# A one-input copy for GpSimd's first weight pass, and the residual stream renewed by VectorE alone

## The reference

```python
# layer 0: Mamba-2 SSD mixer, then an MLP
z, xbc, dt = split(rmsnorm(h, g_pre) @ w_in)        # 2048 | 3072 | 32 columns
xbc = silu(causal_conv4(xbc))                       # depthwise, 4 taps
y, state = ssd(xbc, dt)                             # chunked for the prompt, one step per sample
g = group_rmsnorm((y + x * d) * silu(z)) * gate
h = h + rmsnorm(g @ w_out, g_post)
h = h + rmsnorm(relu(rmsnorm(h, g_pre) @ w_up) ** 2 @ w_down, g_post)
# shared keys and values, once
k, v = split(rmsnorm(h, g_kv) @ w_kv); k = rope(k)
# layer 1: differential attention with its own queries, then an MLP of the same form
h = h + rmsnorm(subln(attn(q, k, v)) @ w_o, g_post)
h = h + rmsnorm(relu(rmsnorm(h, g_pre) @ w_up) ** 2 @ w_down, g_post)
```

## Time and profile before

| | |
|---|---|
| median of 3 runs | 1827.74 us (1825.21 to 1828.12) |
| profiled execution | 1827.72 us |
| its span, first to last instruction | 1825.9 us |
| mean granted clock of TensorE, share of full | 0.923 |
| busy: PE, DVE, ACT, POOL | 1577.9, 1266.2, 469.1, 1332.7 us |
| HBM read, written | 142.07 MB, 16.16 MB |

### The profile page before, as it was taken

One profiled execution on the slowest core, in us unless ns is written; L12 is line 12 of the kernel. 1 busy time (PEld: TensorE's weight loads), 2 busy tenths in 40 slices (PEclk: granted clock), 3 DMA queues, 4 the chain that ended last, 5 costly groups with the idle time before them and its releaser, 6 DMA issues.

```text
span 1825.9 us, 29727 instructions
## 1 busy us (share of the span) xinstructions
PE 1577.9 (86%) x11978; PEld 1479.8 (81%) x11978; DVE 1266.2 (69%) x1075; ACT 469.1 (26%) x1158; POOL 1332.7 (73%) x586
## 2 busy tenths in 40 slices
PE   5999888876499699999997699976769799999995
PEld 5999656876489699999997599953349799999995
DVE  6899888799941698018845936998862996038645
ACT  3433322555621321002100311125542321002100
POOL 5878588556568789888887766644418788888885
PEclk8999999988699799999999799978879799999997
DMA  4222000244423133333333123442212133323321
GB/s 146 75 83 85 18 6 12 105 173 150 150 58 92 47 91 86 92 89 92 92 93 104 45 60 116 135 179 93 70 47 81 47 92 91 92 87 91 92 90 47
DMA packets 44151, 159.40 MB, mean 87 GB/s; under 512 B 5026, under 2 KB 5410, under 8 KB 43810
## 3 DMA queue, kind: packets, MB, share of 16 engines
q1 hardware_dynamic: 44066, 158.25, 27.4%
HBM read 142.07 MB, written 16.16 MB: 87 GB/s over the span
## 4 chain that ended last, share of the span: by engine, by line
PE 55%; DVE 32%; issue 6%; ACT 3%; POOL 2%; DMA 1%; SPq 0%; DVEq 0%; POOLq 0%; ACTq 0%
PE GP L495 17%; PE GP L497 17%; PE GP L496 17%; DVE cacc L1274 4%; DVE hT L1376 2%; DVE acc L1396 2%; DVE hc L1336 2%; DVE hs L1333 2%; DVE kq L1473 1%; DVE aL L1371 1%; DVE hs L1330 1%; DVE decay L1293 1%; DVE misc L1517 1%; DVE hst L1305 1%; DVE yss L1337 1%
## 5 line engine op out<-in xcount | busy, mean ns | idle before, releaser
L405 POOL TENSOR_TENSOR wH<-wraw,cst 128x1024 fp32r<-128x1024 f32 x216 | 532.7, 2466 | 325.6 <-PE GP L497 315.4
L495 PE MATMUL GP<-aH,wH 128*128 128x260 f32 x1920 | 559.9, 292 | 89.4 <-DVE aL L1371 35.2
L409 POOL TENSOR_TENSOR wL<-wraw,wH 128x1024 fp32r<-128x1024 f32 x216 | 576.4, 2668 | 17.0
L497 PE MATMUL GP<-aH,wL 128*128 128x260 f32 x1920 | 553.5, 288 | 0.0
L496 PE MATMUL GP<-aL,wH 128*128 128x260 f32 x1920 | 552.8, 288 | 0.0
L495 PEld LDWEIGHTS GP<-aH,wH 128*128 128x128 f32 x1920 | 373.3, 194 | 98.3 <-issue 49.6
L495 PE MATMUL GP<-hidH,wH 128*128 128x260 f32 x1536 | 440.8, 287 | 8.0 <-DVE hidL L1347 7.3
L497 PE MATMUL GP<-hidH,wL 128*128 128x260 f32 x1536 | 435.9, 284 | 0.0
L496 PE MATMUL GP<-hidL,wH 128*128 128x260 f32 x1536 | 434.9, 283 | 0.0
L496 PEld LDWEIGHTS GP<-aL,wH 128*128 128x128 f32 x1920 | 373.8, 195 | 0.1
L497 PEld LDWEIGHTS GP<-aH,wL 128*128 128x128 f32 x1920 | 373.4, 194 | 0.0
(11 more groups left out here) (255 smaller groups left out, 2041.9 us busy)
## 6 DMA issues: line engine op xcount, KB each, us to landing
wraw<-wblk SPq DMA_DIRECT2D x216, 512.0 KB, 3.6
hs<-ssm_in SPq DMA_DIRECT2D x16, 512.0 KB, 3.7
sssm<-hs SPq DMA_DIRECT2D x16, 512.0 KB, 2.8
ktile<-kcache SPq DMA_DIRECT2D x16, 512.0 KB, 3.6
vtile<-vcache SPq DMA_DIRECT2D x16, 512.0 KB, 4.5
hT<-x_t SPq DMA_DIRECT2D x4, 520.0 KB, 5.1
kt_out<-kT SPq DMA_DIRECT2D x1, 2080.0 KB, 6.6
vt_out<-vT SPq DMA_DIRECT2D x1, 2080.0 KB, 10.6
```

The source lines that it names most:

```text
L405: pool.tensor_tensor(wH[:, d, :].rearrange("p (k n) -> p k n", k=8), raw[:, s, :].rearrange("p (k n) -> p k n", k=8), cst[:, C_ONE:C_ONE + ...
L409: pool.tensor_tensor(wL[:, d, :], raw[:, s, :], wH[:, d, :].bitcast(F32), ALU.subtract).then_inc(w_lo, 1)
L495: pe.matmul(out, lh, rh, start=first, stop=False)
L497: return pe.matmul(out, ll, rh, start=False, stop=last)
```

## The change

Three edits. The first weight pass on POOL becomes a copy with one input instead of a product with ones. The splits are written out one by one for all 216 blocks, without loops. `scale_output` is gone: DVE itself forms `fT = fT * gain * rpost` in one instruction, one tile ahead, and then `hT = hT + fT` in a second.

```diff
-            pool.tensor_tensor(wH[:, d, :].rearrange("p (k n) -> p k n", k=8),
-                               raw[:, s, :].rearrange("p (k n) -> p k n", k=8),
-                               cst[:, C_ONE:C_ONE + 1, :].broadcast_to([P, 8, P]), ALU.mult).then_inc(w_hi, 1)
+            pool.tensor_copy(wH[:, d, :], raw[:, s, :]).then_inc(w_hi, 1)
             pool.wait_ge(w_hi, i * RAW + (s + 1))
             pool.tensor_tensor(wL[:, d, :], raw[:, s, :], wH[:, d, :].bitcast(F32), ALU.subtract).then_inc(w_lo, 1)
...
         def stream(a, b):
-            while a < b and (a % RAW or a == 0 or b - a < RAW):
...
-                with pool.Fori(a // RAW, a // RAW + m) as i:
-                    for s in range(RAW):
-                        split(i, s, False)
...
             for j in range(a, b):
-                split(j // RAW, j % RAW, False)
-
-        def scale_output(p):
-
-            pool.wait_ge(rp_s, p + 1)
-            for m in range(KT):
-                pool.tensor_tensor(fT[:, m, :], fT[:, m, :], rpost[:, :], ALU.mult).then_inc(fr_s, 1)
+                split(j // RAW, j % RAW, j < RAW)
...
             stream(at_, BLOCK0[nxt] + SPL)
             at_ = BLOCK0[nxt] + SPL
-            scale_output(p)
...
         stream(at_, NBLK)
-        scale_output(3)
...
+            def scaled(m):
+                STT(fT[:, m, :], fT[:, m, :], pc(gpost, m), rpost[:, :], ALU.mult, ALU.mult).then_inc(fr_s, 1)
+
+            v.wait_ge(rp_s, p + 1)
+            scaled(0)
             for m in range(KT):
+                if m + 1 < KT:
+                    scaled(m + 1)
                 v.wait_ge(fr_s, 8 * p + m + 1)
-                STT(hT[:, m, :], fT[:, m, :], pc(gpost, m), hT[:, m, :], ALU.mult, ALU.add).then_inc(h_n, 1)
+                TT(hT[:, m, :], hT[:, m, :], fT[:, m, :], ALU.add).then_inc(h_n, 1)
                 if m and p < 3:
                     lows(m - 1)
```

More of the change, by code:

```diff
@@ L412, in stream @@
         def stream(a, b):
-            while a < b and (a % RAW or a == 0 or b - a < RAW):
[L415 to L420, removed]
-                with pool.Fori(a // RAW, a // RAW + m) as i:
-                    for s in range(RAW):
-                        split(i, s, False)
-                a += m * RAW
-            for j in range(a, b):
-                split(j // RAW, j % RAW, False)
-        def scale_output(p):
-            pool.wait_ge(rp_s, p + 1)
-            for m in range(KT):
-                pool.tensor_tensor(fT[:, m, :], fT[:, m, :], rpost[:, :], ALU.mult).then_inc(fr_s, 1)
+            for j in range(a, b):
+                split(j // RAW, j % RAW, j < RAW)
         stream(0, SPL)
```

## The result

The changed kernel takes **1758.20 us** (median of 4 runs, 1753.94 to 1761.49), the kernel before beside it 1827.93 us: ratio 0.9619, 95% interval 0.9595 to 0.9643, 69.7 us less. The forecast was 1789 us (1764 to 1814).

The account below looks back on a forecast made before the run. VectorE, held by GpSimd's current instruction, was taken to set the pace in some stages, TensorE in the GEMMs. Gains of 12 + 8 + 4 + 1.7 + 2 + 8 + 3 = 38.7 us off 1827.7 gave 1789 us, range 1764 to 1814.

Parts of the forecast that it names:

- What bounds, and the lock: DVE sets the pace in some stages because its two-input instructions stand until POOL's current instruction is over.
- I apply 23% to the time that DVE is held, stage by stage.: Copy saves 1.08 of POOL's 4.73 us per block, 23%; DVE's held time was taken to shrink equally.
- z: Gate GEMM with sample states: 59 us of DVE's 148 busy were holding; 12 us gain taken.
- The shared K/V: K/V lows and sums at 1023 us: 17.2 us of DVE time held, 4 us gain.
- the start: Eight scalings (L1186) at the beginning: 7.5 us held by two pairs of weight passes, 1.7 us gain.
- The convolution: Convolution stage: POOL and DVE in series fall from 6.8 to 5.75 us per block; 10 us at most, 8 taken.
- The copy's price: First weight pass on POOL: one copy estimated at 1.26 us, bounds 0.18 and 2.34 us.
- The renewal: POOL's products moved to DVE: 8 us over three layer boundaries, 3 us at the last boundary.
- The stream written out: All 216 splits without loops on POOL: taken as 0, upper bound 5 us of stalls.
- Rival 1: First pass on POOL: the copy is no shorter than the product, 1817 us; chance 0.12.
- rival 3: First pass on POOL: converting makes the copy slower, at 3.1 us the kernel takes 1868 us; chance 0.06.
- Rival 2: First pass on POOL: the copy holds no DVE instruction, half the held time goes, 1766 us; chance 0.12.

Follow-up runs that it names:

- half product: Changed kernel with a two-input product with ones over half of each block (512 elements, wrong weights) as first pass instead of the copy: 1761.93 us.
- no copy: Changed kernel with the two-input product put back as first pass, written-out splits and DVE's boundary work kept: 1815.40 us, ratio 0.9941 against the kernel before.

## Why the prediction was wrong

**What bounds, and the lock: right.** DVE set the pace where the forecast said, because it stood behind POOL's current instruction; the first table above shows it to about 2 us. In the forecast's own window, 330 to 490 us, the same count gives 61.2 us held where the forecast had 59.

**The step that failed: "I apply 23% to the time that DVE is held, stage by stage."** It takes held time to shrink with POOL's time per block. Measured in z, POOL's busy time fell by 25% (88.1 to 65.7 us) and the held time by 38% (60.2 to 37.2). The table by pass shows where: the second pass holds as much as before (27.3 and 27.9 us), and all of the gain is the first pass's. Its instruction got shorter by 56% (2.34 to 1.04 us), the time that it holds by 74% (31.8 to 8.2). Each of the 16 products held a DVE instruction, for 1.99 us in the mean; of the 16 copies 11 did, for 0.75 us each. So length counts twice: a shorter instruction is met less often, and when it is met, less of it is left. (The DVE instruction came 0.41 us after the start of the product in the mean, and 0.43 after that of the copy.) At the very length of the forecast, 1.26 us, the half product shows the same: 46% shorter, but 64% less held (11.4 us). The shared K/V fell by 45% (17.2 to 9.5 us held, its rows from 970.18 to 990.21 us; 7.7 us won where 4 were forecast), the start by 35% (7.5 to 4.8). Some 40% where the forecast has 23% makes z 24, K/V 6.9, start 3.0: 16 of the missing 35 us. What share of short instructions is met isn't settled here: it was 11 of 16 copies, 48 of 64 quarters and 24 and 29 of 32 halves in the kernel before.

**Sizes that were off.** The convolution won 12.6 us where 10 was called the most: it had been reckoned over the earlier trace rows's window, which leaves out both ends of the stage. Over the whole stage PE stood idle for 14.6 us before and 7.8 after, and its busy time fell from 157.9 to 152.1. Attention, MLPs and SSD scan were put at nothing and gave 10.6 us together; that it is the copy's is shown for attention and MLP 0 (column "no copy"), which of their waits gave way isn't; the scan's 1.8 us come without the copy too. For MLP 0 and 1, PE's 5.75 us per block did cover POOL, as forecast: 4.2 us of 681. The copy's price was off by 0.22 us, which by the half product is worth 4 us; the forecast gave the same 4 us.

The Trainium skill (GPSIMD Engine Reference, Engine selection) had one-input work at about line rate, from which the forecast had worked out 1.03 us; this trace agrees, 1.037 us at the shortest.

**The renewal: right, a little small.** 13.6 us alone, 11 forecast. VectorE at the first boundary of the changed kernel:

```profile
565.31 1.43 DVE L1354 SCALAR_TENSOR_TENSOR fT<-fT,pv,rpost 128x520 f32<-128x520 f32 x2 [3.59 <-ACT rpost L871]
566.66 0.69 DVE L1362 TENSOR_TENSOR hT<-hT,fT 128x520 f32<-128x520 f32 x1
567.27 0.75 DVE L1354 SCALAR_TENSOR_TENSOR fT<-fT,pv,rpost 128x520 f32<-128x520 f32 x1
...
579.60 1.63 DVE L1350 SCALAR_TENSOR_TENSOR aL<-hT,pv,aH 128x520 fp32r<-128x520 f32 x2
```

and GpSimd there:

```profile
582.62 1.04 POOL L405 CAST wH<-wraw 128x1024 fp32r<-128x1024 f32 x1 [21.45 <-PE GP L476]
```

The lows end at 581.23, 15.9 us after rpost (forecast 16.2, before 19.5), in steps of 0.61 to 0.68 us, with POOL standing still throughout, as argued. Three boundaries and the end gave 3.5, 2.7, 3.7 and 3.5 us.

**The stream written out: right**, nothing (1.0006).

**The rivals.** Rival 1, the copy no shorter, and rival 3, slower, fall to the 1.04 us. Rival 2, the copy holds nobody, has the nearest time (1766) and the wrong reason: the copy holds (the sum at 359.43 us; 20 us for a second copy). It came close because it took one of two passes to hold nothing, and the first pass's holding did fall by 74%. The range ended just below it, at 1764: the lower bound of the copy's price had been run through the same rule of proportion, and the rule itself had been given no bounds. Of what would show it, the shorter convolution and state instructions (L1274, L1333 and L1336 from 1.76, 1.87 and 2.13 us in the mean to 1.28, 1.52 and 1.54), the boundary's 16 us, 0.67 us steps and no wait for wL came as written; the first pass was shorter than written (1.04 for 1.26), and z (148 forecast over the window of 160 us, 133 by the like window) and acc (5 forecast, 2.2) went further the same way.

## What to carry to other kernels

Where VectorE's two-input instructions (here the one-input scalings L1186 too) share a stage with GpSimd, look first at how long GpSimd's single instructions are, not at its busy share, and add up what VectorE's instructions take over their shortest: where VectorE sets the pace, that sum is what can be won. Shortening the first pass paid more than in proportion here; cutting the second paid until GpSimd, with the fixed costs of the pieces and its own standing at each cut, kept TensorE waiting: 1758 us whole, 1743 in halves, 1736 in quarters, 1754 in eighths. Before cutting, compare GpSimd's new time per unit of work with the engine that it must keep up with elsewhere: 6.06 us against TensorE's 5.75 turned the same cut into a loss of 0.9%.

## What the runs showed of the hardware

- GpSimd's price by size (shortest of each profile): two inputs 0.443, 0.715, 1.26 and 2.34 us for 128, 256, 512 and 1024 elements per partition; one input, rounding to fp32r, 0.600 and 1.03 to 1.04 us for 512 and 1024, so 0.85 ns per element against 2.1.
- The hold goes both ways: a copy that came 0.1 us after a VectorE instruction of 1.22 us took 2.02 us instead of 1.04. Short POOL pieces are lengthened by it too (halves: 1.76 us behind a VectorE instruction, 1.257 at the shortest).
- A GpSimd instruction held at most one VectorE instruction: in the z stages of 13 profiles 542 stands, each behind a GpSimd instruction of its own. Of 16 passes of 2.3 us or more all 16 held one, of 16 copies of 1.04 us 9 to 12.
- Writing out all of GpSimd's 432 weight passes, long runs of which were loops before, cost nothing that can be measured: ratio 1.0006 (0.9993 to 1.0019).
